# Up projections on activations without the token's factor, and the gate as one ScalarE function

## The reference

```python
def conv_ffn(h, w_up, conv_w, conv_b, w_down):
    a = causal_dwconv(h @ w_up, conv_w, conv_b)    
    gate, val = jnp.split(a, 2, axis=-1)
    return (jax.nn.silu(gate) * val) @ w_down

h = h + conv_ffn(rmsnorm(h, norm_ffn[layer]), ...)   # rmsnorm: h * rsqrt(mean(h^2) + eps) * gain
```

## Time and profile before

| | |
|---|---|
| median of 3 runs | 2163.05 us (2162.97 to 2163.73) |
| the profiled execution: its time | 2161.42 us |
| its span, first to last instruction | 2159.7 us |
| mean granted TensorE clock | 0.980 |
| TensorE matmuls busy | 2057.3 us (95%) |
| VectorE busy | 1602.3 us (74%) |
| ScalarE busy | 983.2 us (46%) |
| POOL busy | 609.9 us (28%) |
| up loop of layer 0, of layer 1 | about 510 to 972 us, 1444 to 1906 us |

### The profile page before, as it was taken

The page is one execution under the profiler, slowest core; times in us unless marked ns, Lnnn a source line. Parts: engine busy times, 40 slices in busy tenths (PEclk is TensorE's granted clock), DMA queues, the critical chain, the costliest instruction groups (busy, mean ns, idle before and its releaser), DMA issues.

```text
span 2159.7 us, 39918 instructions
## 1 busy us (share of the span) xinstructions
PE 2057.3 (95%) x13014; PEld 1787.2 (83%) x13014; DVE 1602.3 (74%) x2333; ACT 983.2 (46%) x1391; POOL 609.9 (28%) x686
## 2 busy tenths in 40 slices
PE   5999999989999999999999978989999999999997
PEld 4778877878888888888888877878888888888886
DVE  7786555768888888888777676778888888865655
ACT  5443344444444444445555413544444444444442
POOL 8982100780000000009888574510000000001221
PEclk9999999999999999999999989989999999999999
DMA  4555443454666555557778884545565565556664
GB/s 167 166 167 165 146 135 119 156 165 146 210 218 209 187 187 189 186 185 215 227 236 233 267 252 134 192 135 187 186 190 186 187 194 188 186 185 196 189 180 139
DMA packets 147160, 398.78 MB, mean 185 GB/s; under 512 B 23184, under 2 KB 48400, under 8 KB 147104
## 3 DMA queue, kind: packets, MB, share of 16 engines
q1 hardware_dynamic: 126176, 379.17, 55.8%
q10 hardware_dynamic: 20928, 18.88, 2.7%
HBM read 377.02 MB, written 18.87 MB: 183 GB/s over the span
## 4 chain that ended last, share of the span: by engine, by line
PE 46%; DVE 30%; issue 14%; DVEq 3%; ACT 2%; POOL 1%; DMA 1%; ACTq 1%; POOLq 0%
PE bank L325 22%; PE bank L324 11%; DVE lo L305 11%; DVE cgv L1193 5%; DVE cgv L1190 3%; DVE sumt L339 3%; DVE th L1404 2%; ACT lowt L334 1%; DVE cgv L1403 1%; PE bank L1628 1%; PE bank L1630 1%; PE bank L1629 1%; DVE aa L1408 1%; PE bank L321 1%; DVEq L1193 1%
## 5 line engine op out<-in xcount | busy, mean ns | idle before, releaser
L325 PE MATMUL bank<-xx,hi 128*128 128x512 f32 x3420 | 1203.3, 393 | 0.0
L324 PE MATMUL bank<-xx,lo 128*128 128x256 f32 x3420 | 959.2, 280 | 0.4 <-DVE lo L305 0.4
L305 DVE TENSOR_TENSOR lo<-raw,hi 128x1024 fp32r<-128x1024 f32 x698 | 881.0, 1293 | 103.3 <-ACT hi L298 101.9
L298 ACT ACTIVATE hi<-raw 128x1024 fp32r<-128x1024 f32 x698 | 710.7, 1053 | 336.6 <-PE bank L325 249.8
L325 PEld LDWEIGHTS bank<-xx,hi 128*128 128x128 f32 x3420 | 643.8, 188 | 133.9
L324 PEld LDWEIGHTS bank<-xx,lo 128*128 128x128 f32 x3420 | 647.0, 189 | 11.8 <-DVE lo L305 0.8
L325 PE MATMUL bank<-aa,hi 128*128 128x512 f32 x1344 | 467.7, 392 | 0.0
L324 PE MATMUL bank<-aa,lo 128*128 128x256 f32 x1344 | 376.1, 280 | 4.0 <-DVE lo L305 4.0
L325 PEld LDWEIGHTS bank<-aa,hi 128*128 128x128 f32 x1344 | 252.3, 188 | 54.4
L324 PEld LDWEIGHTS bank<-aa,lo 128*128 128x128 f32 x1344 | 252.4, 188 | 6.6 <-DVE lo L305 5.2
L1193 DVE SCALAR_TENSOR_TENSOR cgv<-sumt,par,cgv 128x255 f32<-128x255 f32 x368 | 180.6, 491 | 54.4 <-DVE cgv L1193 26.1
(11 more groups left out here) (333 smaller groups left out, 1953.1 us busy)
## 6 DMA issues: line engine op xcount, KB each, us to landing
raw<-in_up SPq DMA_DIRECT2D x344, 512.0 KB, 3.9
raw<-in_down SPq DMA_DIRECT2D x160, 448.0 KB, 4.1
raw<-in_w_in SPq DMA_DIRECT2D x98, 512.0 KB, 4.2
raw<-in_w_out SPq DMA_DIRECT2D x32, 512.0 KB, 3.3
raw<-in_down SPq DMA_DIRECT2D x32, 512.0 KB, 3.6
raw<-in_glu SPq DMA_DIRECT2D x32, 512.0 KB, 3.7
s_c<-cp ACTq DMA_DIRECT2D x16, 256.0 KB, 5.0
s_p<-ut ACTq DMA_DIRECT2D x32, 128.0 KB, 5.1
```

Source lines behind the costliest of these rows:

```text
L298: A.activation(hi[:, s, :], raw[:, s, :], ACT.Copy).then_inc(hi_done, 1)
L305: V.tensor_tensor(lo[:, s, :], raw[:, s, :], hi[:, s, :].bitcast(f32), SUB).then_inc(lo_done, 1)
L324: TE.matmul(bank[:, L:], lo[:, s, w], x2[:, k, 0, :], start=False, stop=False)
L325: last = TE.matmul(bank[:, :], hi[:, s, w], x2[:, k, :, :], start=False, stop=k == total - 1)
```

## The change

1. **Activations of the up projections are h * gain.** `gain_high` (ScalarE) and `gain_low` (VectorE) split one tile of h * gain behind each residual tile of w_out or glu; the first up tile is made by the ordinary `pe_tile`, which waits for the tiles in groups. `pe_norm` stands ahead of row block 10 of the first up tile, `pe_norm_wide` ahead of row block 6 of the second.
2. **The token's factor comes after the product**: VectorE multiplies `sumt` by the spread factor in PSUM, in place (`scale`).
3. **The first tap with bias is on ScalarE** (`first_tap`, Identity with scale and bias), and waits for the scaled sum.
4. **The gate is ScalarE's Silu**, and `product` one multiplication.
5. **Order in the loop**: each pair's product, and its split, belong to the same turn now, and the weight splits run one block further ahead of them.
6. **Memory**: w_out reads `aa` instead of `xx`, up 1 reads `aa[8:24]`, whose results go to `xx` for these 16 tiles; the S5 operands are laid out anew, and SyncE loads u before p and the rotations.
7. **ScalarE in w_out**: the wait for `rot_new` and the two mirror copies stand ahead of the last two pairs' splits.

```diff
+XA = 8
+            uu = ph("uu", [P, 4, 4, 4, C5])
             p_op = ph("p_op", [P, SLOTS, 4 * 2, S5_N])
...
+        x_up = (xx, aa[:, XA:XA + KT, :, :])
...
+        def gain_high(a, layer, k, done, value):
+            a.wait_ge(done, value)
+            A.activation(xh_of(layer)[:, bass.ds(k, 1), :], h[:, bass.ds(k, 1), :], ACT.Copy,
+                         scale=par[:, bass.ds(COLS[f"g_ffn{layer}"] + k, 1)]).then_inc(xh_new, 1)
+        def gain_low(v, layer, k):
+            v.wait_ge(xh_new, KT // 2 + layer * KT + k + 1)
+            V.scalar_tensor_tensor(xl_of(layer)[:, bass.ds(k, 1), :], h[:, bass.ds(k, 1), :],
+                                   par[:, bass.ds(COLS[f"g_ffn{layer}"] + k, 1)],
+                                   xh_of(layer)[:, bass.ds(k, 1), :].bitcast(f32), MUL, SUB).then_inc(xl_new, 1)
...
             freed(1)
+            load_u(0)
+            load_u(1)
+            freed(3)
             for kt in range(SLOTS):
                 load_p(kt)
                 load_rot(kt)
-            freed(3)
-            load_u(0)
-            load_u(1)
...
-            with a.Fori(1, KT // 2) as i:
-                act_split(a, B_OUT + LEAD, 4, i, range(4))
+            gain_high(a, 0, 0, tile_read, Q_OUT + 1)
+            def out_pair(i):
+                act_split(a, B_OUT + LEAD, 4, i, range(2))
+                gain_high(a, 0, 2 * i - 1, tile_read, Q_OUT + 2 * i)
+                act_split(a, B_OUT + LEAD, 4, i, range(2, 4))
+                gain_high(a, 0, 2 * i, tile_read, Q_OUT + 1 + 2 * i)
+            with a.Fori(1, KT // 2 - 2) as i:
+                out_pair(i)
             a.wait_ge(rot_new, 1)
-            for x, sign in ((rot_c, 1.0), (rot_s, -1.0)):
-                ins = A.activation(x[:, :, 1:MID], x[:, :, C5 - 1:MID:-1], ACT.Copy, scale=sign)
-            ins.then_inc(rot_whole, 1)
+            A.activation(rot_c[:, :, 1:MID], rot_c[:, :, C5 - 1:MID:-1], ACT.Copy)
+            out_pair(KT // 2 - 2)
+            A.activation(rot_s[:, :, 1:MID], rot_s[:, :, C5 - 1:MID:-1], ACT.Copy, scale=-1.0).then_inc(rot_whole, 1)
+            out_pair(KT // 2 - 1)
...
+                def up_pair(i, to, at, last=False):
                     low_half(a, q_up, b_up + 2 + 4 * i)
+                    act_split(a, b_up + LEAD + 3, 4, i, range(0, 1))
+                    first_tap(i, 0, cg)
+                    if not last:
+                        act_split(a, b_up + LEAD + 3, 4, i, range(1, 2))
                     a.wait_ge(conv_new, 8 + 2 * layer * FT + 1 + 2 * i)
-                    A.activation(th[:, 0, :], cg[:, :], ACT.Tanh, scale=0.5).then_inc(tanh_done, 1)
+                    A.activation(th[:, 0, :], cg[:, :], ACT.Silu).then_inc(tanh_done, 1)
                     low_half(a, q_up + 1, b_up + 4 + 4 * i)
+                    if not last:
+                        act_split(a, b_up + LEAD + 3, 4, i, range(2, 3))
+                    first_tap(i, 1, cv)
+                    if not last:
+                        act_split(a, b_up + LEAD + 3, 4, i, range(3, 4))
+                    high(i, to, at)
...
+                def scale(i, m):
+                    v.wait_ge(tile_read, q_up + 1 + m + 2 * i)
+                    x = sumt[:, (q_up + m) % 2, :]
+                    V.tensor_tensor(x, x, pb[5][:, L:], MUL).then_inc(scaled_new, 1)
...
                 def product(i):
+                    v.wait_ge(conv_new, 8 + 2 * layer * FT + 2 + 2 * i)
                     v.wait_ge(tanh_done, 24 + layer * (FT + KT) + 1 + i)
-                    chain(V.scalar_tensor_tensor(cg[:, :], th[:, 0, :], 1.0, cg[:, :], ADD, MUL))
-                    V.scalar_tensor_tensor(th[:, 1, :], cg[:, :], 0.5, cv[:, :], MUL, MUL).then_inc(a_new, 1)
+                    V.tensor_tensor(th[:, 1, :], th[:, 0, :], cv[:, :], MUL).then_inc(a_new, 1)
...
+                def first_rows(k):
+                    if k in (0, 4, 8, 12, 14, 15):
+                        p.wait_ge(xl_new, KT // 2 + layer * KT + {0: 4, 4: 8, 8: 12, 12: 14, 14: 15, 15: 16}[k])
+                    if k == 10:
+                        pe_norm(p, n)
+                def second_rows(k):
+                    if k == 6:
+                        pe_norm_wide(p, n)
+                pe_tile(p, b_up, 4, 0, 0, q_up, 0, two, up_at[layer], always, first_rows)
+                pe_tile(p, b_up, 4, 0, 2, q_up + 1, 0, two, up_at[layer], always, second_rows)
```

More of the change, by code:

```diff
@@ L306, in dve_split, with pe_tile @@
                                 SUB).then_inc(lo_done, 1)
-        def pe_tile(p, b0, n, i, j0, q, q_i, blocks, x2, ready):
+        def pe_tile(p, b0, n, i, j0, q, q_i, blocks, x2, ready, step=None):
             bank = acc[q % 2]
@@ L940, in up_pair, with first_tap @@
[L940 to L943, removed]
+                act_split(a, b_up + LEAD, 4, 0, range(2, 3))
+                def first_tap(i, m, o):
+                    a.wait_ge(scaled_new, 2 * layer * FT + 1 + m + 2 * i)
+                    if not isinstance(i, int) or i > 0:
+                        a.wait_ge(a_new, layer * FT + i)
+                    base = COLS[f"up{layer}"] + 8 * i + 4 * m
+                    A.activation(o[:, :], sumt[:, (q_up + m) % 2, :], ACT.Identity,
+                                 scale=par[:, bass.ds(base + 2, 1)],
+                                 bias=par[:, bass.ds(base + 3, 1)]).then_inc(tap_new, 1)
@@ L1421, in ffn, with up_pair @@
-                up_pair(0, True)
-                with chain.loop(1, FT, 5) as i:
-                    up_pair(i, False)
-                product(FT - 1)
-                low(FT - 1)
+                    V.tensor_tensor(to[:, bass.ds(i - at, 1), 1, :], th[:, 1:2, :],
+                                    to[:, bass.ds(i - at, 1), 0, :].bitcast(f32), SUB).then_inc(al_new, 1)
+                def up_pair(i, to, at, last=False):
+                    whole(i, 0)
+                    if isinstance(i, int) and i == 0:
+                        dve_split(v, b_up + LEAD + 3, 4, i, range(0, 1))
+                        dve_spread(v, n)
+                        scale(i, 0)
+                    else:
+                        scale(i, 0)
+                        dve_split(v, b_up + LEAD + 3, 4, i, range(0, 1))
+                    taps(i, 0, cg)
+                    if not last:
+                        dve_split(v, b_up + LEAD + 3, 4, i, range(1, 2))
+                    whole(i, 1)
+                    scale(i, 1)
+                    if not last:
+                        dve_split(v, b_up + LEAD + 3, 4, i, range(2, 3))
+                    taps(i, 1, cv)
+                    product(i)
+                    if not last:
+                        dve_split(v, b_up + LEAD + 3, 4, i, range(3, 4))
+                    low(i, to, at)
@@ new lines, in ffn @@
+                up_pair(0, aa, 0)
+                if layer == 0:
+                    with chain.loop(1, FT - 1, 2) as i:
+                        up_pair(i, aa, 0)
+                else:
+                    with chain.loop(1, XA, 2) as i:
+                        up_pair(i, aa, 0)
+                    with chain.loop(XA, XA + KT, 2) as i:
+                        up_pair(i, xx, XA)
+                    with chain.loop(XA + KT, FT - 1, 2) as i:
+                        up_pair(i, aa, 0)
+                up_pair(FT - 1, aa, 0, last=True)
```

172 lines of the change are left out of this document (82 added, 90 removed).

## The result

The changed kernel takes 2140.71 us (median of 4 runs, 2138.49 to 2142.69), the kernel before 2163.01 beside it (4 runs, 2160.50 to 2163.73): 0.9899 of the time, 95% interval 0.9882 to 0.9916, or 22.3 us faster. Forecast were 2137.2 us and a range of 2131 to 2146.

What follows compares the result with a forecast made beforehand. TensorE was taken to set the up loops' pace, so gains lay where it stood still, at the two up-stage starts. 13.5 + 12.3 = 25.8 us off 2163.05 gave 2137.2 us; range 2131 to 2146.

Steps and rivals of the forecast that it cites:

- First start: Start of the first up stage, behind w_out: 19.9 us lost before, 7.6 still lost after, so 12.3 us gained.
- the stall at tile 13: In w_out, TensorE waits because ScalarE's splits queue behind its earlier wait for rot_new: 4.5 us, between 3.1 and 7.3.
- the clock behind it: Matmuls at the lower clock level after the pause in w_out: 1.6 us lost, from 0 to 3.
- the norm: Norm sum and spreading matmul, now inside the first up tiles: 1.5 us for both.
- POOL's squares just in time: First start: POOL's sum of squares, ready at 478 to 482.5, is wanted at 482.9, so 0 us of waiting.
- The 3.4 that I gave for POOL's squares without the stall: First start: TensorE's wait for POOL's sum of squares if w_out did not stall, 480.19 - 476.83 = 3.4 us.
- gain splits in w_out and glu: 0: New splits, 0.42 us a tile on ScalarE and VectorE, fit beside VectorE's 3.3 of 5.57 us: no cost.
- Second start: Start of the second up stage, behind the glu: 15.2 us lost before, 1.7 after (0.17 waiting, 1.5 norm), 13.5 gained.
- Up loops: 86 pairs: VectorE at 9.2 us and ScalarE at 5.5 stay under TensorE's 11.13 a pair, so 0 us change.
- Rival E: ScalarE reloads its function table twice each pair between Identity and Silu: 137 us slower, about 2272; chance 0.05.
- Rival D: VectorE's order of work binds the up loop, 11.25 us a pair against 11.13: 10 us more, 2147; chance 0.05.
- S5 part: SyncE's reordered loads, u before p and rotations: 0 us, 1 each way if a late load meets TensorE.

Runs made afterwards that it cites:

- e5: The changed kernel run again with no edit, on the chip of two later follow-up runs: 2139.55 us, 0.9907 of the kernel before.
- e1: Changed kernel with ScalarE's wait for rot_new and both mirror copies put back behind all w_out splits: 2143.08 us, 0.9926 of the kernel before.
- e2: Changed kernel with, in the glu only, VectorE's low half with gain moved behind the sum, into its wait for tanh: 2139.22 us, 0.9905 of the kernel before.
- e3: Changed kernel without POOL's squares of tiles 1 to 14 for the second layer's norm (norm factor wrong): 2132.95 us, 0.9885 of the kernel before.
- e6: Changed kernel with, in the glu, VectorE's gain half in its wait for tanh and ScalarE's behind both weight splits: 2135.39 us, 0.9884 of the kernel before.
- e4: Changed kernel with the first tap back on VectorE and the tanh gate restored, in both layers: 2143.71 us, 0.9933 of the kernel before.

## Why the prediction was right, and where it was not

The change gained 22.3 us by the medians, 25.8 were forecast. In the profiled execution the two starts gave 20.0 of the 25.8; in e5's trace, of the same kernel, 12.1 + 9.0 = 21.1. The mechanism forecast for the first start came true; at the glu and the second start a step failed, and the range held because it was wide enough for that, not because it had foreseen it.

*First start: gain 12.3 forecast, 12.6 measured.* The mechanism and each term came out: the stall at tile 13 (4.5 forecast, 4.4), the clock behind it (1.6; 1.7), the norm (1.5; 1.3), POOL's squares just in time (0; 0). `rot_new` came 0.6 us earlier against the tiles, where I had weighed 1.9 earlier against up to 4.2 later; that 4.5 then fell so near was in part luck, since the range of the stall was 3.1 to 7.3. The 3.4 that I gave for POOL's squares without the stall was too small: e1 shows a wait of 5.73 and 2.9 us more loss in all.

*Glu: "gain splits in w_out and glu: 0" was the step that failed.* It cost 3.1 us. I added up VectorE's busy time, 3.3 of 5.57, and took the rest for room. The 3.3 was short to begin with, since it left out the sum (0.42) and what POOL does to the splits: in the kernel before VectorE is busy 37.74 of 50 us there (1350 to 1400), 4.2 a tile. And room is not the pace less busy time, since VectorE sits inside a ring: it waits for tanh (0.79) and for its own results. The trace of before shows the room itself, as its wait for lowt ahead of the sum; VectorE, in the glu:

```profile
1390.23 0.42 DVE L339 TENSOR_TENSOR sumt<-bank,lowt 128x256 f32<-128x256 f32 x1 [0.43 <-ACT lowt L334]
...
1392.68 2.78 DVE L305 TENSOR_TENSOR lo<-raw,hi 128x1024 fp32r<-128x1024 f32 x2
1395.80 0.42 DVE L339 TENSOR_TENSOR sumt<-bank,lowt 128x256 f32<-128x256 f32 x1 [0.34 <-ACT lowt L334]
```

The room was about 0.4 us, not 2.3. The new instruction takes 0.48 us, not 0.42, and beside POOL's squares for the coming norm 0.82, which is more than the room. Behind it lay a second limit, the wait for ScalarE's split behind h, which shows only once VectorE's round is shorter (0.61 in e2, 0.20 in e3). In w_out the same step held, with tiles at 5.57, but only just: there the new instruction took 1.28 to 1.51 us in the tiles from 441 to 454, and VectorE had no wait left in them.

*Second start: 1.7 forecast, 4.7 measured, and this follows from the glu.* The forecast took the last square from the trace before, done 3.65 us behind the point at which the first up tile could start. With VectorE behind in the glu it ended 5.1 us behind that tile's start, so the wait was 1.6 instead of 0.17 and the clock fell (1.7), a term that the forecast had at nothing here. In e6, with the glu's pace mended, it ends 3.5 behind and there is no wait. Gain for glu and second start together: 13.5 forecast, 7.4 measured, and 15.2 - 1.6 = 13.6 in e6, so the forecast's size was there to be had.

*Up loops: 0 forecast, 0 measured.* The first tap was mis-sized, 0.60 us for 0.42, inside ScalarE's room: ScalarE's busy time over the span rose by 120.9 us (983.2 to 1104.1) where I gave 72, and the 172 first taps alone are 104 of it. Silu, 0.41, was at the low end of its bounds. Rival E did not come: the loops have no table loads. (Its 84 x 1.6 is 134, not 137; the 2272 is right.) Rival D did not come either: VectorE's room is 1.35 us a pair where I had worked out 0.9. e4 shows where D begins, with 1.25 us more a pair.

*S5 part: 0 within 1 forecast, 1.2 gained in this pair of traces.* In other traces of kernels with the same S5 part the distance moves by several us either way (the changed kernel again: 2.3 shorter), so nothing is to be read into it.

The Trainium skill (SBUF — State Buffer, Who interferes with whom) says that a VectorE instruction with two SBUF inputs contends with a GpSimd instruction that reads SBUF. The runs agree for the new instruction also: L411 takes 0.48 us in e3's glu, and 0.70 to 0.85 beside POOL's squares in the glu of the changed kernel. Where POOL's square starts inside VectorE's split (at 1390.28, in 1390.05 to 1391.26) it takes 1.46 us where its like takes 0.61 alone, so it stood for most of what was left of the split, as the prediction had it. I had drawn on this rule for w_out only; it spoke just as much against the glu.

## What to carry to other kernels

Room on an engine is not the pace less its busy time. Where the engine is one link of a ring, follow one round from start to start, with its waits and with what its neighbours stretch, before an added instruction is priced at nothing; and place it where the engine waits anyway, on both engines that do its halves. A wait moved earlier can pay for itself if it lets a slower engine catch up: undo it only together with what was late behind it. Where a deferred factor makes room, put the small matmuls that need it behind the row block at which their inputs are ready.

## What the runs showed of the hardware

An ACTIVATE on 128x256 with scale and offset both read from SBUF takes 603 ns (L974), one with the gain alone 0.51 us (L405), one with neither 0.41 (L989). The Trainium skill (ScalarE: Activation LUTs, What ACT_TABLE_LOAD costs) gives 186 ns plus 0.833 ns an element plus about 93 ns for each such operand, which makes an estimate of 585, 492 and 399; the rows agree within 20 ns, and the first tap's price could have been had from there.

Identity, Copy and Silu ran in the loop without a table load between them; one load of 1.28 us stood ahead of the first Silu of each stage.

Behind a pause of 1.7 us at the same place the granted clock fell to 1.2 GHz for 3.4 us in one execution of the changed kernel (1.7 us lost) and stayed at 2.4 GHz in another (e5). In e2 it stayed, in e1 and e4 it fell, in e4 for about 6.8 us.
